# Eight gather slots and two weight places, in a two-layer diffusion backbone whose time goes to expert gathers

## The chip, the cores and the metric

One NeuronCore of a Trainium2 chip runs the whole program. The metric is the device time of one execution in microseconds (us), as the median of several. Its engines run side by side, each with its own instruction stream, and wait for each other on semaphores: TensorE (PE) multiplies matrices, VectorE (DVE) and ScalarE (ACT) do the elementwise work, GpSimd (POOL) and SyncE (SP) issue transfers here. All transfers go through the same 16 DMA engines of the core.

## The reference, cut to what matters

256 context tokens and 512 latent tokens of width 1024 (float32) pass two layers. A layer is a mixer and an expert feed-forward (PEER):

```python
for layer in range(DEPTH):                      # DEPTH = 2
    m_lat, m_ctx = mixer(...)                   # layer 0: retention + short convolution; layer 1: windowed attention
    h = h + gate1 * m
    tokens = modulate(rmsnorm(h), shift2, scale2)
    h = h + gate2 * peer_ffn(tokens, wq, keys1, keys2, u_tab, v_tab)
return rmsnorm(h_lat)

def peer_ffn(x, ...):                           # x: (T, 1024)
    # routing: 8 heads pick 16 of 16384 experts for every token, with a softmax gate
    ub, vb = u_tab[expert], v_tab[expert]       # (T, 8, 16, 1024) each
    act = gelu(einsum('td,thkd->thk', x, ub))
    return einsum('thk,thkd->td', gate * act, vb)
```

Every token needs 128 rows of `u_tab` and of `v_tab`, its own ones. The tables are laid side by side on the host, so one row of the joined table `uv` has 2048 floats, 8 KB. Layer 0 does this for 768 tokens, layer 1 for 512 (context tokens drop out): 1280 x 128 rows of 8 KB.

## The kernel before, in words

**Stages.** A stage for the modulation rows of layer 0, a stage for the mixer of layer 0, then `trunk_stage`, in which both expert layers and the whole mixer of layer 1 run, then a final norm. The change lies in `trunk_stage`.

**The gather ring.** A tile is 128 tokens. There are `RUN` = 10 tile passes (six of layer 0, then four of layer 1), each of `TS` = 128 slots; a slot is one expert of every token of the tile. For slot n, numbered through from 0 to 1279:

- POOL issues one indirect DMA of 128 rows of 8 KB, 1 MB, into `ring[:, n % RING]` (line 1198). Before it, it waits until slot n - RING has been used by PE (line 1197, semaphore `slot_free`).
- DVE waits for the landing and makes the dot product of the `u` half with the tokens (`dot`, line 1711).
- ACT turns it into a diagonal matrix: Gelu (line 1246), then the gate (line 1250, `weight`).
- PE multiplies the `v` half with this matrix and adds it up in PSUM (`combine`, line 1441, eight matrix instructions), and frees the slot.

`RING` is 7, and each place has 8 KB on every partition. `diag` and `u` have one place per ring slot too.

**What runs beside the slots.** Each engine's program is a loop over tile passes and slots, and other work is put behind certain slots of it, in an order written out by hand. In this text (4,22) is slot 22 of tile pass 4, counted from 0. The routing of the next tile on DVE and its query products on PE (line 1411) go this way, and so does the mixer of layer 1: norms (`NORMS`), products with the input weights (`PRODUCTS`, line 1481), attention of four blocks of 128 queries (`ATTENDS`: from (4,50), (5,30), (6,50) and (7,8), five slots for a pair of heads), and the output products (`outputs`, line 1572). An engine runs its list strictly in order, so a wait of a mixer instruction also stops the slots behind it.

**The mixer's weights.** They come in pieces of 4 KB on each partition, 512 KB, made of two row blocks (`WG` = 2), four pieces (`PER`) for each product of 512 columns. In all 68 pieces are loaded, by SP, in the order of their use. Piece n goes to `w[n % W_RING]`, and its load waits until piece n - W_RING has been used (`mix_w_used`, line 1097). `W_RING` is 4: two places lie in the modulation rows' buffer (`mod_rows_sb` in the profile), two in `peer_mix_w`. The single loop of SP also holds other loads in fixed places between the pieces: modulation rows and gate rows (line 1112), the query weights and keys of layer 1 (lines 1141 and 1143). PE waits for a piece where it first uses it (line 1452). Products of one tile use a piece in 1 1/3 slots, products of two tiles in 2 2/3, output products in 1 1/3. DVE, too, waits for `mix_w_used` where it reads a product (`keys_roped`, `queries_roped`, `outputs`).

**The other place of `RING`.** In POOL's mixer program the scaling of the probabilities stands at `ATTENDS[b] + STEP * m + 8 + RING` (line 1181), so behind the gather that waits for the combine of slot `ATTENDS[b] + STEP * m + 8`.

Of the kernel before, what the change touches and what calls it, by code (L numbers as in the profile page):

```python
# [15 lines left out]
P = 128  # L16
# [8 lines left out]
HALF = 512  # L25
# [5 lines left out]
NEG = -1e30  # L31
NH, NK, TOPK = 8, 128, 16
EXPERTS = NK * NK
RING = 7
PR = 4
LAG = 2
TAKEN = -3.0e38
# [379 lines left out]
def peer_buffers(arena):  # L417

    cuts = Arena(arena[:])
    return cuts.cut(KC, D), cuts.cut(NH, NK)  # L420
# [545 lines left out]
WG = 2  # L966
# [3 lines left out]
ATTENDS = (at(4, 50), at(5, 30), at(6, 50), at(7, 8))  # L970
PAIRS = ATT_HEADS // 2
STEP = 5
W_RING = 4


def product_slot(job, n):
# [31 lines left out]
def trunk_stage(nc, S, A, h, ident, mod_d, arena, rows, mix_in, mix_out):  # L1008


    with ExitStack() as ctx:
        def sb(name, shape, dt=F32):
            return ctx.enter_context(nc.sbuf_tensor("peer_" + name, shape, dt))

        def sem(name):
            return S("peer_" + name)

        ring = sb("ring", [P, RING, 2 * D])
        wq, keys = peer_buffers(arena)
        shift_row, scale_row, gate_row, mix_gate = rows[:, 0, 0], rows[:, 0, 1], rows[:, 0, 2], rows[:, 1, 0]  # L1020
        w_own = sb("mix_w", [P, 2, WG, HALF])
        w = [rows[:, 1, 1 + x].rearrange("p (k n) -> p k n", n=HALF) for x in range(2)] + [w_own[:, x] for x in range(2)]
        f = sb("f", [P, 2, D])
        fT = sb("fT", [P, KC, P])
        q = sb("q", [P, D])
        sc = sb("scores", [P, 2, NH // 2, NK])
        diag = sb("diag", [P, RING, ROWS])
        stack = sb("stack", [P, ROWS])
# [17 lines left out]
        gate = sb("gate", [P, 2, NH, TOPK])  # L1046
        u = sb("u", [P, RING])

# [40 lines left out]
        def _(sp):  # L1089
            pieces = 0  # L1090

            def next_slot():
                nonlocal pieces
                n = pieces
                pieces += 1
                if n >= W_RING:
                    sp.wait_ge(S("mix_w_used"), n - W_RING + 1)
                return w[n % W_RING], S(f"mix_w{n % W_RING}")

# [56 lines left out]
        def _(pool):  # L1156
# [11 lines left out]
            def mixer():  # L1168
# [5 lines left out]
                for b in range(LT):  # L1174
# [5 lines left out]
                    for m in range(PAIRS):  # L1180
                        yield ATTENDS[b] + STEP * m + 8 + RING
                        p = b * PAIRS + m
# [8 lines left out]
            for i in range(RUN):  # L1191
                for s in range(TS):
                    n, (hd, k) = i * TS + s, divmod(s, TOPK)
                    if k == 0:
                        pool.wait_ge(sem("idx"), i * NH + hd + 1)
                    if n >= RING:
                        pool.wait_ge(sem("slot_free"), n - RING + 1)
                    pool.indirect_dma_start(ring[:, n % RING], None, A["uv"], bass.IndirectOffsetOnAxis(idx[:, i % 2, hd, k:k + 1], 0)  # L1198
# [198 lines left out]
        def _(pe):  # L1397
# [49 lines left out]
            def piece(k, first):  # L1447
# [3 lines left out]
                if first and k % WG == 0:  # L1451
                    pe.wait_ge(S(f"mix_w{n % W_RING}"), 16 * (n // W_RING + 1))
                return w[n % W_RING][:, k % WG]

# [476 lines left out]
def backbone(nc, A, out):  # L1931
    with ExitStack() as ctx:
        S = Sems(nc, ctx)
        mod_d = nc.dram_tensor("mod_rows", (DEPTH, 2, 2, 3, D), F32).ap()
        h = ctx.enter_context(nc.sbuf_tensor("h", [P, NT, D], F32))
        ident = ctx.enter_context(nc.sbuf_tensor("ident", [P, P], F32))
        arena = ctx.enter_context(nc.sbuf_tensor("arena", [P, KC * D + NH * NK], F32))
        rows_flat = ctx.enter_context(nc.sbuf_tensor("mod_rows_sb", [P, 2 * 3 * D], F32))
        rows = rows_flat[:].rearrange("p (a b n) -> p a b n", a=2, b=3)
        strips_d = nc.dram_tensor("decay_strips", (P, RET_HEADS, SL + SC), F32).ap()  # L1940
        silu = ctx.enter_context(nc.sbuf_tensor("silu", [P, 2, KC], F32))
        modulation_stage(nc, S, A, h, ident, silu, mod_d, strips_d, arena, rows_flat)
        mix_in = nc.dram_tensor("mix_in", (3, PER, P, WG, HALF), F32).ap()
        mix_out = nc.dram_tensor("mix_out", (2, PER, P, WG, HALF), F32).ap()
        mixer0_stage(nc, S, A, h, ident, silu, mod_d, strips_d, arena, rows, mix_in, mix_out)
        trunk_stage(nc, S, A, h, ident, mod_d, arena, rows, mix_in, mix_out)
        final_stage(nc, S, A, h, out)
# [38 lines left out]
```

## Time and profile before

| | us |
|---|---|
| median of 3 runs | 3959.76 (3954.98 to 3969.98) |
| the profiled execution, its own time | 3956.97 |
| its span, first to last instruction | 3955.1 |
| PE busy | 2850.4 (72%) |
| DVE busy | 2573.2 (65%) |
| POOL busy | 1593.4 (40%) |
| ACT busy | 1365.7 (35%) |

The profile shows one execution. Busy time of an engine says how long it had an instruction running. The rate of transfers (GB/s) stands beside it for any stretch. A group of instructions is shown by its line in the kernel, the engine, the names of the tiles it writes and reads, and how long its engine sat idle before it, with whoever ended that idle time.

### The profile page before, as it was taken

To read this page: it belongs to the slowest core of one execution; us is meant where nothing else is said; L and a number is where in the kernel's file an instruction comes from. 1 tells how busy PE (TensorE), PEld (TensorE's weight loads), DVE (VectorE), ACT (ScalarE), POOL (GpSimd) and SP (SyncE) were. 2 spreads that over 40 slices of the span, in tenths; PEclk is the share of its full clock that TensorE was granted. 3 is DMA by queue.
4 is the path that set the end of the run, shared out by engine and by line. 5 is a ranking of instruction groups with operands and counts; after the bars stand their busy time and mean duration, and the time that the engine had idled before them with its cause. 6 is when DMAs were issued, how large, how long until landed. Compare 5 with 4: busy or idle time off the path is not lost. (4 is left out here: it accounts for less than half of the span.)

```text
span 3955.1 us, 41286 instructions
## 1 busy us (share of the span) xinstructions
PE 2850.4 (72%) x14677; PEld 976.8 (25%) x14677; DVE 2573.2 (65%) x5990; ACT 1365.7 (35%) x3356; POOL 1593.4 (40%) x1439
## 2 busy tenths in 40 slices
PE   4999956667667666765977688678878866666665
PEld 0794611112112111111323133122423311111110
DVE  3313468885885786687477667757775786686444
ACT  2220123333334233233245345333635433233222
POOL 0205024444444444444344445444445444444332
PEclk6999968678678767867978798788878967766666
DMA  9427369999999999999999999999899999999998
GB/s 371 130 88 275 114 260 421 421 412 421 419 418 414 420 416 406 420 416 412 416 394 369 414 420 351 419 420 419 316 415 389 398 421 417 421 419 406 421 421 335
DMA packets 222862, 1488.84 MB, mean 376 GB/s; under 512 B 27296, under 2 KB 27344, under 8 KB 52032
## 3 DMA queue, kind: packets, MB, share of 16 engines
q0 software_dynamic: 187712, 1352.80, 83.8%
q1 hardware_dynamic: 34832, 133.30, 8.8%
q8 instruction: 115, 1.88, 0.2%
q14 instruction: 91, 0.75, 0.0%
q10 hardware_dynamic: 112, 0.11, 0.0%
HBM read 1480.77 MB, written 15.83 MB: 378 GB/s over the span
## 5 line engine op out<-in xcount | busy, mean ns | idle before, releaser
L1441 PE MATMUL peer_py<-peer_ring,peer_diag 64*64 64x512 f32 x10240 | 1825.1, 811 | 983.1 <-ACT peer_diag L1250 925.2
L1198 POOL DMA_INDIRECT peer_ring<-in_uv_dram,peer_idx x1280 | 1443.6, 1128 | 1920.1 <-PE peer_py L1441 1777.5
L1711 DVE CUSTOM_DVE_ANT_0 peer_ring<-peer_ring,peer_f 128x1024 f32<-128x1024 f32 x1280 | 1557.5, 1227 | 839.2 <-DMA peer_ring<-in_uv_dram,peer_idx 830.6
L1246 ACT ACTIVATE peer_diag<-peer_stack,peer_u 128x64 f32<-128x64 f32 x1280 | 443.8, 347 | 1942.1 <-DVE peer_u L1711 1940.7
L1441 PEld LDWEIGHTS peer_py<-peer_ring,peer_diag 64*64 64x64 f32 x10240 | 349.8, 163 | 2299.2 <-ACT peer_diag L1250 2046.8
L1250 ACT ACTIVATE peer_diag<-peer_diag,peer_gate 128x64 f32<-128x64 f32 x1280 | 445.0, 348 | 46.6
L1411 PE MATMUL peer_pb<-arena,peer_fT 128*128 128x512 f32 x320 | 181.6, 658 | 1.2 <-ACT peer_fT L1218 1.2
L355 DVE TENSOR_TENSOR m_w_low<-m_w_low_plain,m_w_high 128x2048 fp32r<-128x2048 f32 x16 | 37.4, 2337 | 170.8 <-ACT m_w_high L350 170.8
L1796 DVE CUSTOM_DVE_ANT_0 peer_mix_flat<-mix_ps,peer_mix_mask,peer_mix_sink 128x512 f32<-128x512 f32 (+1 forms) x64 | 52.2, 815 | 106.0 <-PE mix_ps L1525 97.8
L1711 DVE DVE_READ_ACCUMULATOR2_ANT peer_u<- 128x1 f32 x1280 | 104.5, 82 | 0.0
L1535 PE MATMUL mix_ps<-peer_mix_flat,peer_mix_v 128*64 128x128 f32 x576 | 97.3, 327 | 0.0
L363 PE MATMUL m_ps<-m_w_high,m_aT_high 128*128 128x512 f32 x240 | 94.8, 395 | 2.7 <-DVE m_v L840 1.7
L363 PE MATMUL m_ps<-m_w_low,m_aT_high 128*128 128x512 f32 x240 | 94.1, 392 | 0.0
L1535 PEld LDWEIGHTS mix_ps<-peer_mix_flat,peer_mix_v 128*64 128x64 f32 x576 | 79.0, 166 | 55.5 <-issue 55.5
L1246 ACT ACT_TABLE_LOAD x66 | 84.7, 1283 | 2.9 <-DVE peer_u L1711 1.8
L350 ACT ACTIVATE m_w_high<-m_w_low_plain 128x2048 fp32r<-128x2048 f32 x16 | 30.7, 1916 | 152.0 <-DMA m_w_low_plain<-in_ev_w_in_dram 104.6
L1411 PEld LDWEIGHTS peer_pb<-arena,peer_fT 128*128 128x128 f32 x320 | 50.4, 193 | 131.1 <-issue 131.1
L1301 ACT ACTIVATE peer_mix_flat<-mix_ps 128x512 f32<-128x512 f32 x64 | 38.0, 594 | 122.2 <-PE mix_ps L1535 67.9
L363 PE MATMUL m_ps<-m_w_high,m_aT_low 128*128 128x512 f32 x192 | 75.4, 393 | 0.0
L363 PE MATMUL m_ps<-m_aT_low,m_w_high 128*128 128x384 f32 x192 | 64.1, 334 | 0.0
L363 PE MATMUL m_ps<-m_aT_high,m_w_high 128*128 128x384 f32 x192 | 64.1, 334 | 0.0
L363 PE MATMUL m_ps<-m_aT_high,m_w_low 128*128 128x384 f32 x192 | 64.1, 334 | 0.0
(210 smaller groups left out, 2624.0 us busy)
## 6 DMA issues: line engine op xcount, KB each, us to landing
mod_rows_sb<-in_ada_w_dram SPq DMA_DIRECT2D x33, 1024.0 KB, 4.9
peer_ring<-in_uv_dram,peer_idx POOLq DMA_INDIRECT x1280, 13.0
arena<-in_ada_w_dram SPq DMA_DIRECT2D x15, 1024.0 KB, 16.1
m_w_low_plain<-in_ev_w_in_dram SPq DMA_DIRECT2D x12, 1024.0 KB, 5.4
mod_rows_sb<-mix_in SPq DMA_DIRECT2D x18, 512.0 KB, 8.8
peer_mix_w<-mix_in SPq DMA_DIRECT2D x18, 512.0 KB, 8.9
arena<-in_peer_wq_dram SPq DMA_DIRECT2D x2, 4096.0 KB, 26.4
mod_rows_sb<-mix_out SPq DMA_DIRECT2D x16, 512.0 KB, 9.4
```

What stands on the lines that cost most here:

```text
L350: act.activation(wh[:, j % 2], wl[0][:, j % 2], ACT.Copy).then_inc(S(tag + "_w_high"), 1)
L355: dve.tensor_tensor(wl[1][:, j % 2], wl[0][:, j % 2], wh[:, j % 2].bitcast(F32), ALU.subtract).then_inc(S(tag + "_w_low"), 1)
L363: ins = pe.matmul(out, l, r, start=j % 2 == 0 and kl == 0 and m == 0, stop=j % 2 == 1 and kl == KH - 1 and m == 2)
L1198: pool.indirect_dma_start(ring[:, n % RING], None, A["uv"], bass.IndirectOffsetOnAxis(idx[:, i % 2, hd, k:k + 1], 0)).then_inc(sem(f"lande ...
L1246: act.activation(diag[:, n % RING], stack[:], ACT.Gelu, scale=u[:, n % RING:n % RING + 1]).then_inc(sem("gelu"), 1)
L1250: act.activation(diag[:, n % RING], diag[:, n % RING], ACT.Copy, scale=gate[:, i % 2, hd, k:k + 1]).then_inc(sem("diag"), 1)
L1301: ins = act.activation(pT[:, 0:HALF], PM[:, 2], ACT.Copy)
L1411: ins = pe.matmul(PB[:, part], fT[:, k], wq[:, k, part * HALF:(part + 1) * HALF], start=k == 0, stop=k == KC - 1)
L1441: ins = pe.matmul(PY[strip(c), r], diag[strip(r), n % RING], ring[strip(r), n % RING, D + c * HALF:D + (c + 1) * HALF], start=s == 0, stop ...
L1535: ins = pe.matmul(out_half(i), v[:, t, 2 * c + x], pT[:, n * P:(n + 1) * P], start=n == 0, stop=n == len(tiles) - 1)
L1711: dve.tensor_tensor_reduce(x, x, f[:, i % 2], 1.0, 0.0, ALU.mult, ALU.add, u[:, n % RING:n % RING + 1]).then_inc(sem("dot"), 1)
L1796: dve.tensor_tensor_reduce(pr[:, i % PR, 0:CTX + n], both_keys(n), mask[:, 0:CTX + n], -SCALE, sink[:, 1, hd:hd + 1], ALU.add, ALU.min, st ...
```

## The change

`RING` becomes 8 and `W_RING` becomes 2. The list of weight places keeps the two in the modulation rows' buffer, and the tile `mix_w` of 8 KB per partition is gone; the ring tile grows by 8 KB per partition.

```diff
-RING = 7
+RING = 8
...
-W_RING = 4
+W_RING = 2
...
         ring = sb("ring", [P, RING, 2 * D])
         wq, keys = peer_buffers(arena)
         shift_row, scale_row, gate_row, mix_gate = rows[:, 0, 0], rows[:, 0, 1], rows[:, 0, 2], rows[:, 1, 0]
-        w_own = sb("mix_w", [P, 2, WG, HALF])
-        w = [rows[:, 1, 1 + x].rearrange("p (k n) -> p k n", n=HALF) for x in range(2)] + [w_own[:, x] for x in range(2)]
+        w = [rows[:, 1, 1 + x].rearrange("p (k n) -> p k n", n=HALF) for x in range(2)]
```

`diag` and `u` grow by one place (256 and 4 bytes per partition). All waits that are written with `RING` or `W_RING` follow.

## Rows read from the trace of the kernel before

**Rows 1.** The page: rate of transfers in 40 equal slices, DMA queues.
```profile
DMA  9427369999999999999999999999899999999998
GB/s 371 130 88 275 114 260 421 421 412 421 419 418 414 420 416 406 420 416 412 416 394 369 414 420 351 419 420 419 316 415 389 398 421 417 421 419 406 421 421 335
...
q0 software_dynamic: 187712, 1352.80, 83.8%
q1 hardware_dynamic: 34832, 133.30, 8.8%
```

**Rows 2.** Stretches: engines' busy us (instructions), granted PE clock, DMA share, GB/s.
```profile
533.00:3932.00 3399.00, 2410.68 (x12535) 670.59 (x12535) 2384.20 (x5708) 1256.34 (x3211) 1504.02 (x1351) 0.77 1.00 408
2043.00:2143.00 100.00, 82.20 (x492) 39.16 (x492) 79.22 (x227) 62.10 (x143) 51.06 (x48) 0.85 0.93 346
2373.00:2453.00 80.00, 67.33 (x425) 32.72 (x417) 65.64 (x180) 46.13 (x118) 39.94 (x38) 0.87 0.91 334
2763.00:2873.00 110.00, 93.00 (x548) 46.81 (x547) 81.98 (x221) 65.76 (x157) 54.47 (x49) 0.83 0.88 323
3023.00:3113.00 90.00, 76.97 (x510) 36.01 (x510) 57.25 (x146) 54.40 (x130) 46.48 (x45) 0.98 0.96 364
1513.00:1543.00 30.00, 17.11 (x108) 3.97 (x100) 18.44 (x30) 11.52 (x31) 13.93 (x14) 0.78 0.98 380
1893.00:1981.00 88.00, 87.89 (x375) 28.46 (x370) 40.02 (x75) 23.45 (x64) 30.22 (x28) 0.97 1.01 415
```

**Rows 3.** The ring's tile between 3640 and 3900 us.
```profile
L1711 DVE CUSTOM_DVE_ANT_0 peer_ring<-peer_ring,peer_f x104: 1224/1225/1227, 3639.7 to 3897.7; 128x1024 f32<-128x1024 f32 x104
...
  DMA peer_ring<-in_uv_dram,peer_idx: 132.1, 104
...
DMA to landing us min/median/max: 12.1/13.1/14.9
```

**Rows 4.** Waits between 2763 and 2873 us: total, times, longest.
```profile
POOL peer_ring L1198 <- PE peer_py L1441: 53.2, 20, 4.3
PEld peer_py L1441 <- ACT peer_diag L1250: 26.9, 14, 4.0
DVE peer_mix_flat L1796 <- PE mix_ps L1525: 24.1, 8, 4.7
ACT peer_mix_flat L1301 <- PE mix_ps L1535: 19.1, 6, 3.8
```

**Rows 5.** The ring's tile in the same stretch.
```profile
L1711 DVE CUSTOM_DVE_ANT_0 peer_ring<-peer_ring,peer_f x36: 1203/1220/1727, 2763.4 to 2871.9; 128x1024 f32<-128x1024 f32 x36
...
  DMA peer_ring<-in_uv_dram,peer_idx: 1.5, 2
...
DMA to landing us min/median/max: 5.4/7.6/10.1
```

**Rows 6.** POOL's timeline at the start of tile pass 3.
```profile
1522.36 1.15 POOL L1198 DMA_INDIRECT peer_ring<-in_uv_dram,peer_idx  x1 [1.40 <-PE peer_py L1441]
1530.65 0.94 POOL L1198 DMA_INDIRECT peer_ring<-in_uv_dram,peer_idx  x1 [7.15 <-PE peer_py L1441]
```

**Rows 7.** PE's timeline of the first block's output products.
```profile
2170.46 3.70 PE L1572 MATMUL mix_ps<-mod_rows_sb,h 128*128 128x512 f32 x8
2174.00 3.60 PE L1572 MATMUL mix_ps<-peer_mix_w,h 128*128 128x512 f32 x8
...
2180.16 1.12 PE L1572 MATMUL mix_ps<-mod_rows_sb,h 128*128 128x512 f32 x2 [1.55 <-DMA mod_rows_sb<-mix_out]
...
2182.24 1.12 PE L1572 MATMUL mix_ps<-mod_rows_sb,h 128*128 128x512 f32 x2
2183.94 1.12 PE L1572 MATMUL mix_ps<-mod_rows_sb,h 128*128 128x512 f32 x2 [0.58 <-DMA mod_rows_sb<-mix_out]
...
2194.95 1.12 PE L1572 MATMUL mix_ps<-peer_mix_w,h 128*128 128x512 f32 x2
```

**Rows 8.** SP's timeline of the same products: issues of pieces.
```profile
2172.47 2.04 SPq L1109 DMA_DIRECT2D mod_rows_sb<-mix_out  x2
2175.91 2.04 SPq L1109 DMA_DIRECT2D peer_mix_w<-mix_out  x2
```

**Rows 9.** PE's timeline, products of tile pass 4 (pieces 8 to 12).
```profile
1894.10 3.78 PE L1481 MATMUL mix_ps<-mod_rows_sb,peer_mix_flat 128*128 128x512 f32 x4
...
1903.04 1.02 PE L1481 MATMUL mix_ps<-peer_mix_w,peer_mix_flat 128*128 128x512 f32 x2
...
1914.77 1.88 PE L1481 MATMUL mix_ps<-mod_rows_sb,peer_mix_flat 128*128 128x512 f32 x4
```

**Rows 10.** Loads and gathers issued from 2622 to 2708 us: us to landing.
```profile
mod_rows_sb<-mix_in SPq DMA_DIRECT2D x4, 512.0 KB, 8.3
peer_mix_w<-mix_in SPq DMA_DIRECT2D x4, 512.0 KB, 7.9
...
peer_ring<-in_uv_dram,peer_idx POOLq DMA_INDIRECT x28, 13.4
```

**Rows 11.** The gathers issued from 1893 to 1981 us.
```profile
DMA to landing us min/median/max: 9.0/14.0/18.2
```

## The prediction

> **What bounds the kernel now.** I read the slices of the page first. From the seventh slice on the DMA engines are busy nine tenths of the time or more, and the rate stands at 406 to 421 GB/s in most slices; it falls to 394, 369, 351, 316, 389 and 398 in six of them [rows 1]; the last slice holds the end of the trunk. So the trunk is limited by how fast gathers arrive, except in places. The plateau is 421 GB/s: between 3640 and 3900 us DVE makes 104 dots in 260 us, 2.5 us each, and waits for a landing before every one of them (132.1 us in all) [rows 3]. The price of one gather at full rate is therefore 2.5 us.
>
> The view of stretches then says how much is missing. From 533 to 3932 us the mean rate is 408 [rows 2], so 3399 x (1 - 408/421) = 105 us of transfer time went unused. The four stretches in the middle of the attention blocks hold most of it: 100 x (1 - 346/421) = 17.8, 80 x (1 - 334/421) = 16.5, 110 x (1 - 323/421) = 25.6 and 90 x (1 - 364/421) = 12.2, together 72 us. The rest, 33 us, is in small dips, those at tile starts among them: 30 x (1 - 380/421) = 2.9 us in the one listed [rows 2].
>
> Who is late in the attention stretches? In the 110 us one DVE waits for gathers 1.5 us in all [rows 5], POOL waits 53.2 us for PE to free a slot, PE 26.9 us for ACT, DVE 24.1 us for PE's transposed probabilities or scores, ACT 19.1 us for PE [rows 4]. A gather lands in 7.6 us there [rows 5], against 13.1 in the full-rate stretch [rows 3]. The gathers are on time and lie in the ring; the engines wait for one another. The change matters in three ways: what an eighth slot buys in the stretches of full rate, what it buys here, and what PE's waits for weight pieces cost.
>
> **The eighth slot.** At full rate 13.1 / 2.5 = 5.2 gathers are on their way at any time and the other 1.8 slots are being worked on. With eight slots it is 6.2, and a landing takes 15.6 us from its issue. This alone moves nothing, since the DMA engines already have work: 421 GB/s stays 421. What it gives is a longer reserve. PE may now fall behind by 15.6 us instead of 13.1 before the DMA engines run dry.
>
> Attention stretches: the ring is full of landed gathers while compute is the slower side, and the transfers stop one ring ahead of PE. With eight slots they stop one gather further ahead, once per stretch, and that gather is already there when the following stretch at full rate begins. Four stretches, each followed by one at full rate: 4 x 2.5 = 10 us gained. The pace inside the stretch is not touched, by rows 4 and 5. Bounds: 0 (if a stretch begins so late that the reserve never fills) and the 72 us that are missing there.
>
> Dips: at the start of tile pass 3 POOL waits 7.15 us for PE, which itself stands until the old tile has been read out [rows 6]. That is less than the 13.1 us of reserve, so the DMA engines should not have been dry, although the rate is 380 [rows 2]. The dip is then not a matter of slots, and an eighth mends little of it. I take -2 us over the nine tile starts; bounds 0 and 9 x 2.9 = -26 us. POOL's scalings of the probabilities (line 1181) keep their place relative to the combine, at no cost.
>
> **Two places for pieces, in the output products.** Before, four pieces lie ready and the other four are issued as places come free. The first is issued at 2172.5 [rows 8] and PE starts on it at 2180.2 [rows 7]: 7.7 us from issue to use. The next starts at 2183.9, 3.8 us later. The eight pieces take PE from 2170.5 to 2196.1, 25.6 us [rows 7], with a good ten slots of combines between the products. With two places only two pieces lie ready, and the six others come in three pairs. A pair needs 7.7 us to land, and its first piece is used for 3.2 us (2180.16 to 2182.24 + 1.12 [rows 7]) before its place can be filled again. So the first piece of the last pair starts at 2172.5 + 7.7 + 2 x (7.7 + 3.2) = 2202.0; the second lands 3.8 later and is used for 3.2: it ends at 2209.0, 13 us late.
>
> Does this reach the end? In these 38.5 us the DMA engines can move 38.5 x 0.421 = 16.2 MB; some seven pieces take 3.7 MB, and 12.5 MB or 11.9 gathers (1.049 MB each) remain, while PE frees some 10.7 slots. The reserve of 6.2 gathers shrinks by 1.2 net, and within one wait of 7.7 us by 2 or 3 more. It does not reach zero, so the product is late and the gathers are not. PE's late work is made up behind it: in full-rate stretches it waits for the gathers anyway. I take 0.5 us for each of four blocks, 2 us. Bounds: 0 and 4 x 13 = 52 us, if the cover is gone.
>
> A piece and a gather lie in different queues. If a piece had to stand behind the gathers queued before it, its 7.7 us would become 10.2 with one more gather ahead. Between 2622 and 2708 us pieces land in 7.9 to 8.3 us while gathers take 13.4 [rows 10], so a piece does not stand behind them. The Trainium skill has the same in "DMA: Bandwidth & Descriptors", section "Queues, rings and completion order": each DMA engine goes round the queues that have work, a packet of each at a time. By that rule 7.7 us stays as it is; by the other reading the last pair would start 3 x 2.5 = 7.5 us later in each block, and four blocks would have 30 us more to hide.
>
> **Two places, in the input products.** Pieces 10 and 11 (tile pass 4) had landed long before their use, and now wait for pieces 8 and 9 to be used. Piece 8 ends at 1897.9 and PE wants piece 10 at 1903.0 [rows 9]; it lands 7.9 later at 1905.8, a delay of 2.8 us. SP stands in line there: the two modulation rows behind piece 11, until now issued earlier, are issued at about 1903 and land in front of piece 12 at 3.8 us apiece. Pieces 11, row, row, 12 land at 1911.1, 1914.9, 1918.7, 1922.5, while PE wants piece 12 at 1914.8 + 2.8 [rows 9]: 4.9 us more. In all PE is 7.7 us late. Later pieces serve two tiles and 2 2/3 slots each, about 8 us, as long as a load, and add nothing. PE is busy 87.89 of 88 us here [rows 2], so the delay stays. What covers it is the reserve: the gather with the least of it landed in 9.0 us [rows 11], where 5.4 is the shortest seen [rows 5]. That leaves 3.6 us, plus 2.5 by the eighth slot: 6.1 against 7.7. I take 2 us; bounds 0 and 7.7. Tile pass 6 has one gate row instead of two modulation rows, so 2.8 + 1.0 = 3.8 us, under its own reserve; passes 2, 3 and 5 lie in full-rate stretches and wait at most 2.8 us. All three: 0, bounds 0 and 3.8 + 2 x 2.8 = 9.4.
>
> SP's other loads come later, but each is wanted a tile pass after its place: the new modulation rows at (5,10), the gate rows at (3,1) and (7,1).
>
> **The sum.** -10 - 2 + 2 + 2 + 0 = -8 us. The profiled execution took 3956.97; less 8 is 3949. The median of the runs stands 2.8 us above the profiled one (3959.76), so I forecast 3952. Its own range is 3935 to 3968.
>
> **The rivals.**
> (a) The pieces are not covered. PE is stopped in its order for 13 us in each output block and 7.7 + 9.4 us in the products; if the DMA engines are dry in that time, it is 52 + 17 = 69 us, less the 10 of the exits: 3960 + 59 = 4019. Half of it gives 3960 + 35 - 10 = 3985. It decides from the point at which PE frees no slot for longer than the gathers under way last. For it: PE was all busy in the products of pass 4, and the reserve there was the smallest. Against it: 12.5 MB of gather capacity against 10.7 slots freed in the output products.
> (b) The ring bounds the attention stretches. With 8 slots for 7 the 380 us of them would take 7/8, 47 us less: 3913; for a third of it, with the tile starts mended, 3930. For it: POOL's wait on PE is the longest row [rows 4]. Against it: DVE's 1.5 us of waiting for gathers [rows 5]. The Trainium skill gives, in "DMA: Bandwidth & Descriptors", section "Anatomy of one DMA", a fixed 2 us for each transfer beside its bytes; more transfers under way would hide more of it. The 421 GB/s with seven slots say that it is hidden already at full rate.
> (c) Nothing moves: gain and waits cancel within 2 us, 3960. It cannot be told from the forecast.
>
> **How the numbers follow.** Forecast and (c) together 0.61, of which 0.01 is faster; (a) in full 0.05, in half 0.09; (b) in full 0.08, in part 0.17. A measurement of this kernel can tell 0.5%, some 20 us, from no change: faster means under 3940, slower over 3980. Faster 0.26, same 0.60, slower 0.14. The range reaches to (b) in part and (a) in half: 3925 to 3985.
>
> **What would show it.** After: gathers at full rate land in about 15.6 us; PE has two waits of some 5 to 8 us in each of three pairs of output pieces, and the block takes about 38 us instead of 25.6, at a rate that stays above 410; the attention stretches keep their pace and have about the same missing time; the stretch of pieces 8 to 19 loses one to four us of transfers. The prediction is wrong if the rate falls under 400 in the output blocks, if the 110 us stretch gets shorter by more than 5 us, or if dips at tile starts vanish.

## The result and the profile after

| | us |
|---|---|
| before, median of 18 runs | 3961.47 (3954.98 to 3970.94) |
| with the change, median of 18 runs | 3978.83 (3966.61 to 3989.94) |
| ratio to before | 1.0043, 95% interval 1.0035 to 1.0051 |
| the profiled execution of the change, its own time | 3985.16 |

The change makes the kernel 17 us slower, where 8 us less were forecast. The profiled executions lie 28 us apart (3956.97 and 3985.16), more than the medians. Eight of these 28 us lie ahead of the trunk, in stages that the change doesn't touch: the first gather is issued at 541.0 us instead of 532.7. The trunk itself is some 20 us longer.

The slices and the wait that was not there before (page and waits of the changed kernel; line numbers are one less from line 1022 on):

```profile
GB/s 370 130 85 277 110 242 421 421 421 421 417 420 413 419 421 401 411 421 420 394 398 383 387 420 363 402 420 406 328 380 400 379 404 421 421 421 420 421 421 326
```
```profile
PEld mix_ps L1571 <- DMA mod_rows_sb<-mix_out: 65.6, 20, 7.5
DVE peer_mix_flat L1744 <- PE mix_ps L1480: 56.1, 8, 10.8
```
```profile
L1197 POOL DMA_INDIRECT peer_ring<-in_uv_dram,peer_idx x1280: 932/940/2001, 541.0 to 3945.7; - x183
```

Twenty waits for output pieces, 65.6 us in all (14.8 us in 7 waits before). The stretches of the changed kernel that answer to [rows 2], moved by what it is late at that point, with the four output blocks and one input product behind them (columns as in [rows 2]):

```profile
541.00:3961.00 3420.00, 2414.63 (x12536) 670.24 (x12540) 2385.07 (x5711) 1255.80 (x3211) 1507.54 (x1351) 0.78 0.99 406
2051.00:2151.00 100.00, 81.87 (x492) 38.39 (x492) 80.41 (x230) 62.65 (x144) 50.06 (x47) 0.85 0.96 365
2382.00:2462.00 80.00, 66.32 (x419) 32.74 (x421) 67.48 (x186) 45.71 (x116) 42.13 (x37) 0.87 0.92 350
2775.00:2885.00 110.00, 91.61 (x534) 45.25 (x534) 82.26 (x231) 66.31 (x159) 54.16 (x47) 0.83 0.89 326
3044.00:3134.00 90.00, 76.97 (x501) 35.80 (x500) 55.80 (x137) 53.48 (x128) 44.49 (x44) 0.96 0.96 369
1516.00:1546.00 30.00, 17.46 (x104) 4.38 (x104) 18.86 (x32) 11.22 (x32) 13.46 (x14) 0.73 0.98 381
1895.00:1991.00 96.00, 87.61 (x370) 28.20 (x370) 41.29 (x77) 24.66 (x66) 29.87 (x28) 0.96 0.99 393
2178.00:2216.00 38.00, 26.67 (x87) 7.62 (x88) 24.19 (x64) 6.95 (x20) 5.73 (x7) 0.82 0.88 346
2500.00:2540.00 40.00, 29.03 (x152) 7.04 (x144) 30.70 (x80) 8.59 (x25) 17.87 (x16) 0.87 0.95 375
2912.00:2950.00 38.00, 26.41 (x77) 7.90 (x75) 22.16 (x58) 6.96 (x20) 5.98 (x5) 0.79 0.85 327
3145.00:3185.00 40.00, 29.26 (x112) 8.00 (x104) 28.53 (x75) 9.04 (x26) 13.33 (x10) 0.81 0.96 381
1585.00:1600.00 15.00, 12.54 (x38) 3.71 (x38) 2.95 (x10) 1.16 (x4) 2.38 (x3) 0.77 0.86 335
```

Transfer time unused, as (1 - rate/421) x length: in the output blocks 6.8 + 4.4 + 8.5 + 3.8 = 23.5 us. These stretches of some 40 us end before the blocks have recovered; over 80 us each block shows more:

| GB/s in 80 us from the start of each output block, about | block 1 | 2 | 3 | 4 | unused, us |
|---|---|---|---|---|---|
| before (from 2165, 2485, 2895, 3125) | 418 | 420 | 420 | 420 | 1 |
| the change (from 2173, 2495, 2907, 3145) | 378 | 397 | 371 | 379 | 30 |

The first block before, in the short stretch:

```profile
2172.00:2210.00 38.00, 27.62 (x122) 7.38 (x124) 27.33 (x71) 7.66 (x22) 11.31 (x11) 0.90 1.02 418
```

In the products of pass 4 it is 6.4 us against 1.3, and in the product of pass 3 3.1 us. Together some 37 us lost. The attention stretches miss 13.3 + 13.5 + 24.8 + 11.1 = 63 us, against 72: 9 us gained. The trunk is only 20 us longer, so some 8 more were gained elsewhere. They lie in the dips. The start of tile pass 1, before, with the change, and with six slots (a run below):

```profile
860.00:890.00 30.00, 17.79 (x108) 4.46 (x112) 18.46 (x31) 10.34 (x29) 13.94 (x13) 0.73 1.00 393
860.00:890.00 30.00, 16.24 (x100) 4.06 (x96) 20.38 (x37) 12.68 (x31) 13.49 (x12) 0.72 1.01 420
860.00:890.00 30.00, 18.67 (x104) 4.68 (x104) 18.88 (x33) 12.59 (x31) 13.01 (x13) 0.67 0.97 377
```

The starts of pass 4 (406 GB/s before, 419 after, 60 us from 1835) and pass 9 (396 before, 419 after, 60 us from 3580 and from 3600) mend in the same way; that of pass 3 does not (380 and 381).

How an output block looks now. PE's and POOL's timelines of the changed kernel around 2180 us:

```profile
2175.55 1.09 PE L1440 MATMUL peer_py<-peer_ring,peer_diag 64*64 64x512 f32 x8 [1.76 <-ACT peer_diag L1249]
2176.57 3.70 PE L1571 MATMUL mix_ps<-mod_rows_sb,h 128*128 128x512 f32 x8
2186.47 6.01 PE L1571 MATMUL mix_ps<-mod_rows_sb,h 128*128 128x512 f32 x8 [6.20 <-DMA mod_rows_sb<-mix_out]
2192.42 1.09 PE L1440 MATMUL peer_py<-peer_ring,peer_diag 64*64 64x512 f32 x8
...
2198.13 1.99 PE L1440 MATMUL peer_py<-peer_ring,peer_diag 64*64 64x512 f32 x8
...
2202.44 1.09 PE L1440 MATMUL peer_py<-peer_ring,peer_diag 64*64 64x512 f32 x8
...
2204.51 1.09 PE L1440 MATMUL peer_py<-peer_ring,peer_diag 64*64 64x512 f32 x8
...
2210.66 1.37 PE L1440 MATMUL peer_py<-peer_ring,peer_diag 64*64 64x512 f32 x8
...
2213.01 1.09 PE L1440 MATMUL peer_py<-peer_ring,peer_diag 64*64 64x512 f32 x8
```
```profile
2176.95 1.15 POOL L1197 DMA_INDIRECT peer_ring<-in_uv_dram,peer_idx  x1 [1.41 <-PE peer_py L1440]
2193.81 0.94 POOL L1197 DMA_INDIRECT peer_ring<-in_uv_dram,peer_idx  x1 [15.71 <-PE peer_py L1440]
2200.42 0.94 POOL L1197 DMA_INDIRECT peer_ring<-in_uv_dram,peer_idx  x1 [5.66 <-PE peer_py L1440]
```

Between the combine at 2175.6 and the next at 2192.4 PE does eight matrix instructions, waits, and does eight more: no slot is freed, and POOL stands for 15.7 us. In the other blocks its longest stand is 17.0, 18.9 and 15.5 us. In the 38.5 us from 2176.6 to 2215.1 PE frees six slots in all. The transfers of the 38 us from 2178, in 40 slices of 0.95 us, are thin from 15 us in and fall to nothing about 22 us in, at 2200. That is at the end of the next stand, of 5.7 us, and not in the long one:

```profile
GB/s 414 414 423 423 388 431 410 431 410 427 418 423 414 423 405 392 194 401 242 276 410 354 43 0 0 112 310 405 388 431 410 423 418 405 457 431 328 332 237 198
```

The order of the program says why the burst is there. The output products are listed from slot 54 behind the block's start (`out_slot`), but the attention program of PE ends at slot 58 (its twelfth round, 5 x 11 + 3), and the products can't begin ahead of its end. So eight of the sixteen, those due by slot 58, run behind one combine (two instructions each, 8 + 8 in the rows above). [rows 7] shows this too: 3.70 and 3.60 us of products in one piece from 2170.46, before a combine. With four places that burst finds its four pieces loaded; with two places it has a full load in its middle.

### The profile page after: what moved, and what is told of

Read it like the earlier page. It is cut to its first block and busy times, and to the rows that moved or that the text cites. A ratio compares the mean times of both kernels' runs of the same rounds, so it can differ in the third digit from the quotient of the medians.

```text
span 3983.3 us, 41286 instructions
## 1 busy us (share of the span) xinstructions
PE 2859.3 (72%) x14677; PEld 980.4 (25%) x14677; DVE 2572.1 (65%) x5990; ACT 1365.5 (34%) x3356; POOL 1596.6 (40%) x1439
## 5 line engine op out<-in xcount | busy, mean ns | idle before, releaser
L1480 PE MATMUL mix_ps<-mod_rows_sb,peer_mix_flat 128*128 128x512 f32 x224 | 116.7, 628 | 17.7 <-DMA mod_rows_sb<-mix_in 17.7
L1795 DVE CUSTOM_DVE_ANT_0 peer_mix_flat<-mix_ps,peer_mix_mask,peer_mix_sink 128x512 f32<-128x512 f32 (+1 forms) x64 | 52.2, 815 | 107.2 <-PE mix_ps L1524 95.3
L1571 PE MATMUL mix_ps<-mod_rows_sb,h 128*128 128x512 f32 x128 | 84.7, 789 | 46.0 <-DMA mod_rows_sb<-mix_out 46.0
```

The lines of the kernel that those rows point to most:

```text
L1480: ins = pe.matmul(PM[:, bank], aT[to][:, k], weights, start=k == 0, stop=k == KC - 1)
L1571: ins = pe.matmul(PM[:, c], qT[b % 2][:, m], weights, start=m == 0, stop=m == PAIRS - 1)
L1795: dve.tensor_tensor_reduce(pr[:, i % PR, 0:CTX + n], both_keys(n), mask[:, 0:CTX + n], -SCALE, sink[:, 1, hd:hd + 1], ALU.add, ALU.min, st ...
```

## The experiments

Each was timed beside the kernel before; the first four in one session (before: 3960.68 us), the last four in a second one (before: 3962.56), so across the two the ratios are compared. Theory A: what costs is the time in which PE frees no slot, once that is about as long as the gathers under way last.

**One half alone: seven slots, two places.**

```diff
-RING = 8
+RING = 7
```

> Seven gather slots with two weight places: the second half of the change alone. Theory A (PE stands for some 16 us without freeing a slot at the start of each output block, longer than the gathers under way last; the eighth slot gives back some 12 us of the loss): the loss is larger with seven slots, about 30 us as with eight, plus 2.5 us in each of four output blocks, without the eighth slot's gain: 3995 to 4005 us. Rival B (the eighth slot gives nothing, or costs): 3979 us or less, as the changed kernel.

Measured: 4001.36 us, ratio to before 1.0098 (1.0080 to 1.0117). That is in A's range. The two places alone cost 40 us, and the eighth slot gives 22 of them back. So the eighth slot is a gain, and the places are the whole of the loss. But A expected 2.5 us more in each output block, 10 in all, and there the seven slots lose hardly more than the eight: 384, 377, 380 and 374 GB/s over 80 us, 32 us unused against 30. So nearly all of the 22 us lie outside the blocks, in the dips and the attention stretches.

**The burst taken apart.**

```diff
 def out_slot(b, n):
-    return ATTENDS[b] + STEP * PAIRS + 14 + 2 * n // 3
+    return ATTENDS[b] + STEP * PAIRS + 18 + 2 * n // 3
```

> The changed kernel, with the output products moved four slots later (first product behind the combine of slot 58 after the block's start, where the attention program ends, and the same pace of 2/3 slot). This undoes the burst of seven products behind one combine and leaves all waits for pieces. Theory A (the loss is the stretch without a combine): the longest stretch in which PE frees no slot falls from 16 to about 8 us, the rate in the output blocks rises from about 340 to over 400 GB/s, and the time falls by 20 to 28 us to 3951 to 3959 us. Rival C (what counts is PE's lateness of 13 us in each block, wherever it stands): 3979 us as the changed kernel.

(It is eight products, as said above, not seven.)

Measured: 3969.19 us, ratio 1.0016 (1.0004 to 1.0027), 10 us less than the changed kernel; 20 to 28 were expected. The intervals leave some 5 us either way on such a difference; the runs of this kernel lie wide, 3954 to 3974, and the profiled one (3961.86) is 7 us below their median. The waits for pieces are all still there, 62.1 us in 17 against 65.6 in 20, and the first 38 us of the block run at full rate. Waits, stretch and POOL's timeline of this kernel:

```profile
PEld mix_ps L1571 <- DMA mod_rows_sb<-mix_out: 62.1, 17, 6.0
```
```profile
2172.00:2210.00 38.00, 25.46 (x88) 6.86 (x88) 28.39 (x72) 11.43 (x28) 10.45 (x8) 0.79 1.02 419
```
```profile
2183.59 1.08 POOL L1197 DMA_INDIRECT peer_ring<-in_uv_dram,peer_idx  x1 [7.03 <-PE peer_py L1440]
...
2196.83 1.06 POOL L1197 DMA_INDIRECT peer_ring<-in_uv_dram,peer_idx  x1 [6.71 <-PE peer_py L1440]
```

POOL now waits 7.0 and 6.7 us instead of once 15.7, and a third time 8.5 us up to 2211.7, behind this stretch. Over 80 us the blocks run at 410, 416, 416 and 390 GB/s: 10 us unused, where the changed kernel has 30. In the fourth block the transfers do stop. POOL's stands there, and the transfers from 3165 to 3205 us in slices of 1 us:

```profile
3150.27 0.94 POOL L1197 DMA_INDIRECT peer_ring<-in_uv_dram,peer_idx  x1 [8.21 <-PE peer_py L1440]
...
3163.15 0.94 POOL L1197 DMA_INDIRECT peer_ring<-in_uv_dram,peer_idx  x1 [6.79 <-PE peer_py L1440]
...
3177.57 1.89 POOL L1197 DMA_INDIRECT peer_ring<-in_uv_dram,peer_idx  x1 [8.49 <-PE peer_py L1440]
```
```profile
GB/s 217 397 426 406 393 451 410 426 410 438 279 57 41 8 0 180 344 426 385 385 401 393 401 410 442 442 410 410 442 451 410 401 451 434 410 410 426 442 418 410
```

No stand is near the 15.6 us of the gathers under way, yet three of them, with too few slots freed between, empty the ring. So A in its plain form, the longest stand alone, is wrong. The edit also changes two things at once: in the first block it cuts the long stand, and it lets PE free ten slots between the first product and the last (2169 to 2214 us) instead of six. These runs don't tell the two apart.

**Burst and pace.**

```diff
-    return ATTENDS[b] + STEP * PAIRS + 14 + 2 * n // 3
+    return ATTENDS[b] + STEP * PAIRS + 18 + n
...
-... (4, 0, at(5, 106)), ...
+... (4, 0, at(5, 110)), ...
```

> The changed kernel, with the output products four slots later and one slot apart instead of 2/3 (a pair of pieces then has 4 slots, some 10 us, for a load of 8 and its use). The norm behind the second block moves from slot 106 to 110. Theory A: PE hardly waits for pieces, 3945 to 3955 us, a little under r8w2_start. Rival C: the same 3945 to 3955 us, since PE isn't late either; so A and C part in the distance to r8w2_start, 0 to 6 us by A, 20 or more by C.

Measured: 3956.30 us, ratio 0.9989 (0.9980 to 0.9997). The distance to the kernel with the burst alone removed is 13 us, between A's 0 to 6 and C's 20 or more. So neither is right alone: of the 23 us between the changed kernel and this one, 10 go with the burst and 13 with the slower pace (32.6 us of waits in 17 are left of 62.1), each within some 5. By the traces the blocks run at 420, 420, 419 and 420 GB/s over 80 us: 1 us unused, after 30 and 10. That puts some 20 us on the first step and 9 on the second.

**The control.** The same two lines in the kernel before (seven slots, four places).

> The kernel before, seven slots and four weight places, with the same moved and spread output products: the control for r8w2_spread. Theory A: the output blocks were no loss before, so 3958 to 3964 us, as before. If it gets faster by over 8 us, the order of the products is worth something by itself and r8w2_spread's gain isn't that of the slot.

Measured: 3962.75 us, ratio 1.0000 (0.9989 to 1.0010). The order of the products alone is worth nothing with four places. The spread kernel is 6 us faster than this one by the medians (4 by the ratios), in spite of its two places; that is the slot.

**Half pieces in four places.** The same 8 KB, cut finer.

```diff
-WG = 2
+WG = 1
...
-W_RING = 2
+W_RING = 4
...
-        w = [rows[:, 1, 1 + x].rearrange("p (k n) -> p k n", n=HALF) for x in range(2)]
+        w = [rows[:, 1, 1 + x // 2, x % 2 * HALF:(x % 2 + 1) * HALF].rearrange("p (k n) -> p k n", n=HALF) for x in range(4)]
```

> The changed kernel with its 8 KB for weights cut into four places of 2 KB and the pieces halved (136 loads of 256 KB in place of 68 of 512 KB), all slots of the products as in the changed kernel. Theory A (what costs is the longest stretch in which PE frees no slot): a smaller piece comes sooner after the place is free, so the stretch at the start of an output block falls from 17 to some 11 us, under the 15.6 us of gathers under way, and the time from 3979 to 3962 to 3970 us. Rival D (the loads' latency is mostly fixed, so that twice as many waits cost as much as before): 3979 us or more.

Measured: 3983.96 us, ratio 1.0058 (1.0045 to 1.0071). My expectation was wrong, rival D's right. PE's timeline shows four half pieces used as they land:

```profile
2180.07 2.07 PE L1571 MATMUL mix_ps<-mod_rows_sb,h 128*128 128x512 f32 x2 [4.65 <-DMA mod_rows_sb<-mix_out]
2183.23 2.08 PE L1571 MATMUL mix_ps<-mod_rows_sb,h 128*128 128x512 f32 x2 [1.09 <-DMA mod_rows_sb<-mix_out]
2186.40 2.08 PE L1571 MATMUL mix_ps<-mod_rows_sb,h 128*128 128x512 f32 x2 [1.10 <-DMA mod_rows_sb<-mix_out]
2189.59 2.08 PE L1571 MATMUL mix_ps<-mod_rows_sb,h 128*128 128x512 f32 x2 [1.11 <-DMA mod_rows_sb<-mix_out]
```
```profile
mod_rows_sb<-mix_out SPq DMA_DIRECT2D x12, 256.0 KB, 8.4
```

They come 3.2 us apart, where whole pieces came 3.8 us apart [rows 7], and in the median they take 8.4 us to land. Half the bytes take nearly the same time, so the burst got longer, not shorter: PE's next combine is at 2191.6, 20 us after its last.

**The input products too.** On top of the spread kernel:

```diff
-    return job[2] + 2 * n // 3
+    return job[2] + (n if len(job[1]) == 1 else 2 * n // 3)
...
-            in_pieces(KV)
+            in_pieces(KV, 0, W_RING)
             sp.wait_ge(sem("f"), NT)
             lat = (1, 1, 1)
             modulation_rows()
+            in_pieces(KV, W_RING, PER)
```

(and the same for the gate row of layer 1; `in_pieces` takes the first and the last piece to load).

> The kernel with eight slots, two places and moved and spread output products, and in addition the products of one tile one slot apart instead of 2/3, and the modulation and gate rows of layer 1 issued before the last two of their four pieces instead of behind them. Theory A: the losses in the input products (4 us at the start of tile pass 3's product, 3 us in pass 4) go, so 3946 to 3951 us against 3956. Rival E (these waits are covered, as was predicted, and the loss there is something else): 3956 us.

Measured: 3952.64 us, ratio 0.9972 (0.9961 to 0.9983), 3.7 us under the spread kernel by the medians, 7 by the ratios. The stretch of the product in pass 3, 335 GB/s in the changed kernel, is at 409:

```profile
1580.00:1595.00 15.00, 14.36 (x60) 4.15 (x59) 5.26 (x10) 3.48 (x10) 5.22 (x5) 1.00 1.01 409
```

As A expected, but for 2 us. The edit changes the pace and the place of the rows together, and their shares aren't known. This kernel beats both: some 10 us under before, 26 under the change.

**Half pieces with all of it.** The half pieces, the spread output products and the earlier rows, with the input products at their old pace.

> Half-size pieces in four places of 2 KB, the moved and spread output products, and the rows issued ahead of the later pieces, with the input products at their old pace. Theory A: hardly any wait for pieces is left, 3944 to 3950 us. Rival D (fixed latency): like the spread kernel or slower, 3956 us or more.

Measured: 3958.01 us, ratio 0.9989 (0.9979 to 1.0000). Expected were 3944 to 3950. Nothing gained by the cut here either.

**What a slot is worth with four places.** The kernel before with `RING = 6`.

> The kernel before with six gather slots in place of seven and its four weight places: what one slot is worth where pieces aren't the matter. By the prediction's sum (one gather at each of four exits from the attention blocks and 2 us in dips) 12 us slower, 3973 us. Theory A with the eighth slot's worth as measured with two weight places (22 us, part of it in the output blocks): 15 to 25 us slower, 3976 to 3986 us. Rival F (a slot is worth more the fewer there are, since the start of each tile then runs dry): over 30 us slower, above 3990 us.

Measured: 3984.19 us, ratio 1.0062 (1.0050 to 1.0074): 22 us slower, in A's range, and nearly twice the 12 of the prediction's sum. The attention stretches, where that sum puts most of it, are no worse: 73 us unused in wide stretches (105 to 140 us each) as with seven slots. The whole trunk leaves 122 us unused against 105, so the 17 more lie in the dips, as at 860 us above (377 GB/s against 393). The full rate is the same, and the landing is one gather earlier, 10.6 us against 13.1 (transfers of this kernel between 3650 and 3900 us):

```profile
DMA packets 14451, 105.29 MB, mean 421 GB/s; under 512 B 1605, under 2 KB 1605, under 8 KB 1605
...
peer_ring<-in_uv_dram,peer_idx POOLq DMA_INDIRECT x100, 10.6
```

Eight slots and four whole places together, the cleanest test of the slot alone, don't fit into the on-chip memory; no run has them.

## Why the prediction was wrong, by its steps

- **The bound** (transfers at 421 GB/s, and 105 us unused) held. The changed kernel runs the last tile at 421 GB/s again with eight slots.
- **The eighth slot, forecast -12 us** (10 in the attention stretches, 2 in the dips), was right in sign, and its parts were mis-sized. The runs give 22 us with two places, and at least the 4 to 6 us between the control and the spread kernel, where waits for pieces are left. In the attention stretches the change gained 9 us, over wide stretches 65 us unused against 73; but the spread kernel has 71 there, and six slots have 73 like seven: the forecast 10 isn't borne out. In the dips it gained some 8 to 11 us where I took 2. I had read one tile start (pass 3, 380 and then 381 GB/s) and taken all nine for its like; those of passes 1, 4 and 9 nearly vanish. By my own signs ("if dips at tile starts vanish") that was a miss.
- **Attention stretches bound by one another's engines, not by the ring** (against rival b): right. POOL waits 52.2 us for PE in the 110 us stretch, DVE makes 37 dots there instead of 36.
- **The output products, forecast +2 us of a possible 52**: this is the step that failed. I took "a good ten slots of combines between the products" and "one wait of 7.7 us" as the longest stand. The 10.7 slots are 16 products x 2/3 slot, the pace of the list; but the first eight are late already and stand behind one combine. So PE frees six slots in the block, before (from 2170.5 to 2196.1 us) and after (in 38.5 us). With 11.9 gathers wanted and six slots freed the reserve of 6.2 shrinks by 5.9 and not by 1.2: the same sum with the right count says that nothing is left. The longest stand is load plus burst, 15.8 us, and the gathers under way last 15.6. My own [rows 7] had the burst in it: two lines of products with no combine between. The block's length itself was right: 38 us forecast, 2176.6 to 2215.1 or 38.5 measured. The cost is 29 us by the rates over 80 us (30 against 1); the runs give 23 us between the changed and the spread kernel.
- **The input products, forecast +2 us**: too small. Pass 4 lost 5 us (the delay of PE, 7.7 us, was foreseen; the waits of piece 10 and piece 12 measure 2.9 and 5.5 us against 2.8 and 4.9 forecast). Pass 3, taken as covered, lost 3 us: PE waits 3.3 us for the third piece, and DVE, which reads the product two slots later, stands 10.2 us for it with dots behind it in its list. I had not counted this second engine: its waits for products of the input weights went from 20.1 to 56.1 us.

PE's wait for piece 6 in pass 3, then for pieces 10 and 12 in pass 4 (three moments of PE's timeline of the changed kernel), and DVE's wait behind the last:

```profile
1587.46 2.08 PE L1480 MATMUL mix_ps<-mod_rows_sb,peer_mix_flat 128*128 128x512 f32 x2 [3.30 <-DMA mod_rows_sb<-mix_in]
...
1905.89 1.12 PE L1480 MATMUL mix_ps<-mod_rows_sb,peer_mix_flat 128*128 128x512 f32 x2 [2.89 <-DMA mod_rows_sb<-mix_in]
...
1923.39 3.78 PE L1480 MATMUL mix_ps<-mod_rows_sb,peer_mix_flat 128*128 128x512 f32 x4 [5.50 <-DMA mod_rows_sb<-mix_in]
```
```profile
1598.21 0.42 DVE L1744 TENSOR_TENSOR peer_mix_flat<-mix_ps,peer_mix_tables 128x256 f32<-128x256 f32 x1 [10.21 <-PE mix_ps L1480]
```

- **A piece does not stand behind the gathers**: right, 7.9 us from the issue at 2178.6 to the use at 2186.5, with one gather more under way.
- **Rival (a)** in half, 3985 us with 0.09, is the nearest of the cases to the 3979 measured. Its condition, PE freeing no slot for longer than the gathers under way last, was named; against it I set "10.7 slots freed", which was wrong. The nearness of 3985 is in part luck: it holds 35 us for waits and 10 for the slot, where the rates show 37 and some 17 to 20.

What stays open: by how much a long stand costs more than the same lateness in short ones. The stands of 15.7, 17.0, 18.9 and 15.5 us exceed the 15.6 by some 5 us together, where 30 are unused; an even balance over the block would leave the ring just empty at its end. Neither gives the 30 alone, and no run keeps the number of slots freed and changes only the stand. Nor is the 13 us between the start and the spread kernel fully placed: their blocks differ by 9, and their profiled executions by only 2 (3961.86 and 3960.10).

## What to carry to other kernels

A ring covers its consumer's lateness until the consumer has caught up, whether that comes in one stand or in several short ones. Before taking away places of a second ring that the same in-order engine waits on, take the instructions of that engine as they ran, and not the pace at which they are listed. Count the slots freed from the first use to the last (six here, not 10.7). Find the longest run without one that frees a slot, add the load that now falls inside it, and compare both with the gathers under way. Read every dip of a kind before calling it no matter of the ring. Where places are scarce, spreading the uses in the list (two lines here) was worth 23 us, while cutting the places finer was worth nothing.

## What the runs showed of the hardware

- **The two queues shared the DMA engines by rows, not by bytes.** At some 421 GB/s in all, whole pieces (rows of 4 KB) next to gathers (rows of 8 KB) came every 3.8 us: 0.524 MB / (3.8 x 0.421 MB per us) = 0.33 of the bytes, 4 of 4 + 8. Half pieces (rows of 2 KB) came every 3.2 us: 0.262 / (3.17 x 0.421) = 0.20, 2 of 2 + 8. One row of each queue in turn gives these shares, and so do equally many rows of each. By this an urgent load beside a saturating one would be faster with longer rows; no run here has them. This is in line with the round by packets in the Trainium skill's "DMA: Bandwidth & Descriptors", section "Queues, rings and completion order"; that the share goes by the number of rows, whatever their size, is what these runs add.
- **At full rate a deeper ring added only latency.** Six, seven and eight slots give 421 GB/s each, with 10.6, 13.1 and 15.6 us from issue to landing (the last from POOL's issues and DVE's dots of the same slots in the changed kernel, and as the median to landing from 3650 to 3900 us in the spread kernel).
